# A hybrid decoder layer: late loads of the delta rule one tile further on, and the sparse branch's first items in another order

## The reference

```python
h = rmsnorm(x); u = h @ w_in
A = conformer_conv(u)                 # causal depthwise conv, w = 31
B = gated_deltanet(u)                 # chunked delta rule, 4 heads of 128
C = sparse_attention(u)               # 8 heads of 64 in 2 groups
x += (sigmoid(gA)*A + sigmoid(gB)*B + sigmoid(gC)*C) @ w_o
x += cross_attention(rmsnorm(x), mem)
x += relu(rmsnorm(x) @ w_ff1)**2 @ w_ff2
```

## Time and profile before

| what | us |
|---|---|
| median of three runs | 2863.49 |
| the three runs | 2863.49, 2866.32, 2855.11 |
| the profiled execution, its own time | 2858.21 |
| its span, first to last instruction | 2856.6 |
| TensorE matmuls busy in it | 2657.9 (93%) |
| VectorE, ScalarE, GpSimd busy | 1311.3, 853.5, 693.3 |
| mean granted clock of TensorE | 0.962 of 2.4 GHz |

### The profile page before, as it was taken

How to read it: one execution, slowest core, us unless ns; L and a number is a source line. 1 busy time by engine, 2 the same in 40 slices (tenths; PEclk the granted TensorE clock), 3 DMA queues, 4 the chain that set the end, 5 groups by cost and what they waited for, 6 DMA issues and landing times. The chain is left out here.

```text
span 2856.6 us, 53065 instructions
## 1 busy us (share of the span) xinstructions
PE 2657.9 (93%) x21974; PEld 2438.0 (85%) x21974; DVE 1311.3 (46%) x2318; ACT 853.5 (30%) x1603; POOL 693.3 (24%) x548
## 2 busy tenths in 40 slices
PE   8999999999889987888879999999999999999996
PEld 7999999999867764545548899988999999999995
DVE  4999999313133346455543352234333323324234
ACT  4333111123122234556652222135221121220221
POOL 1222222212143330121203424201422222222233
PEclk9999999999978897999999999999999999999998
DMA  5121252332386735335316551233111111111111
GB/s 176 53 60 60 98 107 87 92 98 70 110 256 197 212 104 204 119 110 161 119 43 224 145 188 60 74 132 134 48 44 50 45 45 45 45 45 46 50 46 61
DMA packets 148834, 290.35 MB, mean 102 GB/s; under 512 B 28100, under 2 KB 96648, under 8 KB 145842
## 3 DMA queue, kind: packets, MB, share of 16 engines
q1 hardware_dynamic: 136930, 255.48, 28.6%
q0 software_dynamic: 11520, 31.47, 3.5%
q10 hardware_dynamic: 144, 0.00, 0.0%
HBM read 245.94 MB, written 51.93 MB: 104 GB/s over the span
## 5 line engine op out<-in xcount | busy, mean ns | idle before, releaser
L165 POOL TENSOR_TENSOR mlp_w_low<-mlp_w_raw,mlp_w_high 128x1024 fp32r<-128x1024 f32 x72 | 174.5, 2424 | 656.8 <-ACT mlp_w_high L161 656.8
L362 PE MATMUL in_psum<-x_high,in_w_high 128*128 128x352 f32 x1416 | 264.5, 328 | 23.8 <-DVE x_low L557 13.8
L165 POOL TENSOR_TENSOR in_w_low<-in_w_raw,in_w_high 128x1024 fp32r<-128x1024 f32 x59 | 145.4, 2465 | 576.1 <-ACT in_w_high L161 576.1
L2759 PE MATMUL mlp_psum<-mlp_in,mlp_w_high 128*128 128x352 f32 x1536 | 264.9, 324 | 0.0
L161 ACT ACTIVATE mlp_w_high<-mlp_w_raw 128x1024 fp32r<-128x1024 f32 x72 | 76.4, 1061 | 624.2 <-PE mlp_psum L2759 624.2
L362 PEld LDWEIGHTS in_psum<-x_high,in_w_high 128*128 128x128 f32 x1416 | 234.4, 189 | 32.4 <-issue 17.0
L362 PE MATMUL in_psum<-x_low,in_w_high 128*128 128x352 f32 x1416 | 261.8, 327 | 0.0
L362 PE MATMUL in_psum<-x_high,in_w_low 128*128 128x352 f32 x1416 | 259.0, 324 | 0.0
L2759 PEld LDWEIGHTS mlp_psum<-mlp_in,mlp_w_high 128*128 128x128 f32 x1536 | 251.2, 189 | 0.2
L362 PEld LDWEIGHTS in_psum<-x_low,in_w_high 128*128 128x128 f32 x1416 | 237.3, 191 | 0.0
L362 PEld LDWEIGHTS in_psum<-x_high,in_w_low 128*128 128x128 f32 x1416 | 235.1, 190 | 0.0
(11 more groups left out here) (468 smaller groups left out, 4444.8 us busy)
## 6 DMA issues: line engine op xcount, KB each, us to landing
mlp_w_raw<-in_w_mlp SPq DMA_DIRECT2D x64, 512.0 KB, 3.5
in_w_raw<-in_w_in SPq DMA_DIRECT2D x59, 512.0 KB, 4.3
nsa_ring<-in_cache_slc SPq DMA_DIRECT2D x144, 128.0 KB, 3.9
u_scratch<-stage SPq DMA_DIRECT2D x32, 528.0 KB, 5.3
gdnp_page_ring<-in_cache_cmp POOLq DMA_DIRECT2D x128, 128.0 KB, 4.6
gdnp_page_ring<-in_cache_cmp SPq DMA_DIRECT2D x128, 128.0 KB, 4.8
nsa_ring<-in_cache_slc POOLq DMA_DIRECT2D x112, 128.0 KB, 4.1
aux<-u_scratch SPq DMA_DIRECT2D x24, 528.0 KB, 4.2
```

The source lines that it names most:

```text
L165: self.nc.gpsimd.tensor_tensor(self.low[:, i % 2, 0:k * P], self.raw[:, i % 2, 0:k * P], self.high[:, i % 2, 0:k * P].bitcast(F32), ALU.su ...
L362: return mm(psum[:, e % 2, n, 0:WN], w[:, i % 2, c * P:(c + 1) * P], a[:, c, n * WN:(n + 1) * WN], start=x == 0 and c == 0, stop=x == 2 an ...
L2759: return mm(psum[:, e % 2, n, 0:WN], w[:, i % 2, c * P:(c + 1) * P], a(c)[:, column(n)], start=x == 0 and c == 0, stop=x == 2 and c == CHU ...
```

## The change

In the delta rule, GpSimd and SyncE load four page steps first (FIRST = 4), then GpSimd's memsets, first mask product and padding and SyncE's new tokens follow, and then steps 4 and 5. The spill and the sample's inputs move into SyncE's loop at t = 1, behind that tile's token load and ahead of its pages. The transfer of `sample_mask` is gone.

In the sparse branch, the causal mask comes from `sample_consts`: `SC_OWN` has 16 columns instead of 4, `SC_EDGE` four more, and VectorE adds the latter to the window's bias; TensorE's three products with `early.mask` are gone. The past's scores go to banks 4 and 5, so that the 16 transposes wait for less. The preamble's new tokens, importance and past values become functions, called after the scoring of items 0, 1 and 2; ScalarE's and VectorE's counterparts move likewise. Head 0 takes tiles 0 to 7 in order. Both windows come first among the sets. `compare` moves behind item 2 and keeps only the small sums; its large comparisons stand behind items 4 (`larger`) and 6 (`equal`, with the tie-breaking), `count` behind 7, and `masks` before item 9.

```diff
-    STEPS, RING = N_PAGES // 4, 6
+    STEPS, RING, FIRST = N_PAGES // 4, 6, 4
...
+            def load_late():
+                sp.dma_start(spill, conv).then_inc(sent, 16)
+                sp.dma_start(own[:, :], t_dram["sample_own"]).then_inc(own_in, 16)
+                sp.dma_start(state_s[:, :, :, :], t_dram["state_gdn"]).then_inc(state_in, 16)
...
-            for step in range(RING):
+            for step in range(FIRST):
                 load_pages(sp, step, (0, 1), pages_in)
             sp.dma_start(qkv_new[:, :, :], qkvs[:, :, TP:W].rearrange("k p n -> p k n")).then_inc(sample_in, 16)
             sp.dma_start(zs[:, :, :], u[T_Z:T_Z + H, :, TP:W].rearrange("h p n -> p h n")).then_inc(sample_in, 16)
-            sp.dma_start(spill, conv).then_inc(sent, 16)
...
+            for step in range(FIRST, RING):
+                load_pages(sp, step, (0, 1), pages_in)
             for t in range(NT):
                 if t + 2 < NT:
                     load(t + 2)
+                if t == 1:
+                    load_late()
...
-            for step in range(RING):
+            for step in range(FIRST):
                 load_pages(pool, step, (2, 3), pages_in_pool)
...
             last.then_inc(pad_ready, 1)
+            for step in range(FIRST, RING):
+                load_pages(pool, step, (2, 3), pages_in_pool)
...
-    sets = [(x, hf, c) for hf in range(2) for x, c in [(WIN, 0)] + [(SLC, c) for c in range(NCH)]]
+    sets = [(WIN, 0, 0), (WIN, 1, 0)] + [(SLC, hf, c) for hf in range(2) for c in range(NCH)]
-    RANKED = 6
+    RANKED = 9
-        items.append((PROMPT, n // NT, (0, 7, 1, 6, 2, 5, 3, 4)[n] if n < NT else n % NT))
+        items.append((PROMPT, n // NT, n % NT))
...
-                mm(ps[:, b, 0:c1 - c0], early.rbx[:, :], early.hot[:, c0:c1], start=True, stop=False)
-            for k, at in enumerate((C_WIN, C_WIN + WINDOW, C_DIFF + PAGE)):
-                last = mm(ps[:, at // BANK, at % BANK:at % BANK + TS], early.mask[:, 0:P], early.mask[:, P + k * TS:P + (k + 1) * TS],
-                          start=False, stop=k != 1)
+                last = mm(ps[:, b, 0:c1 - c0], early.rbx[:, :], early.hot[:, c0:c1], start=True, stop=True)
...
                 for which, (n, k) in merged(scoring, tailing):
                     (tail if which else score)(n, k)
+                if i == 0:
+                    new_tokens()
+                if i == 1:
+                    importance()
+                if i == 2:
+                    past_values()
...
+            V.tensor_tensor(bias[:, C_WIN:C_WIN + TS], bias[:, C_WIN:C_WIN + TS], piece(SC_EDGE, TS), ALU.add)
...
                 if i >= 1:
                     scales(i - 1)
+                if i == 0:
+                    past_shares()
                 if i == 1:
+                    new_tokens()
+                if i == 2:
                     compare()
-                if i == 3:
+                if i == 4:
+                    larger()
+                if i == 6:
+                    equal()
+                if i == 7:
                     count()
```

More of the change, by code:

```diff
@@ L1516, in sparse @@
     last_of_head = {r: i for i, (kind, r, _) in enumerate(items) if kind == PROMPT}
-    last_set = {hf: item_of_set[hf * (NCH + 1) + NCH] for hf in range(2)}
+    last_set = {hf: item_of_set[1 + (hf + 1) * NCH] for hf in range(2)}
     def spans(tt):
@@ L1782, in _ @@
                 last.then_inc(v_turned, 1)
-            pe.wait_ge(turned, 1)
-            pe.wait_ge(past_ready, 2)
-            for b in range(4):
-                last = mm(ps[strip(b), M1, 0:NCMP], piece(SC_SUM, 32), sc[:, b % 2, :], start=True, stop=True)
-            last.then_inc(imp_mm, 1)
-            for hf in range(2):
-                tr(ps[:, 4 + hf, P:2 * P], sc[:, hf, :], ident[:, :]).then_inc(past_turned, 1)
-            for hf in range(2):
-                pe.wait_ge(past_pt, hf + 1)
-                for b in range(HB):
-                    last = mm(ps[strip(b), 4 + hf, 0:P], pt[:, hf, 0, strip(b)], vc_past[:, hf * HB + b, :], start=True, stop=True)
-                last.then_inc(past_pv, 1)
@@ new lines, in importance, with past_values @@
+            def importance():
+                pe.wait_ge(turned, 1)
+                pe.wait_ge(past_ready, 2)
+                for b in range(4):
+                    last = mm(ps[strip(b), M1, 0:NCMP], piece(SC_SUM, 32), sc[:, b % 2, :], start=True, stop=True)
+                last.then_inc(imp_mm, 1)
+                for hf in range(2):
+                    tr(ps[:, 4 + hf, P:2 * P], sc[:, hf, :], ident[:, :]).then_inc(past_turned, 1)
+            def past_values():
+                for hf in range(2):
+                    pe.wait_ge(past_pt, hf + 1)
+                    for b in range(HB):
+                        last = mm(ps[strip(b), 4 + hf, 0:P], pt[:, hf, 0, strip(b)], vc_past[:, hf * HB + b, :], start=True, stop=True)
+                    last.then_inc(past_pv, 1)
+                pe.wait_ge(past_out, 2)
+                tr(ps[0:NC, 4, 0:P], vct[:, :], ident[:, :]).then_inc(vc_turned, 1)
+                pe.wait_ge(m0_read, 1)
@@ L1882, in _ @@
             act.wait_ge(v_turned, 2)
-            act.activation(vtok[:, 1, :, :], ps[:, 2:4, :], ACT.Copy).then_inc(v_ready, 1)
+            act.activation(vtok[:, 0, :, :], ps[:, 0:2, :], ACT.Copy).then_inc(v_ready, 1)
+            for i in range(LAG - 1):
+                for _ in exps(i):
+                    pass
+                if i == 0:
+                    act.wait_ge(turned_mm, 1)
+                    act.activation(vn[:, :, :, :].rearrange("p a b n -> p (a b n)"), ps[0:NEW, M1, :], ACT.Copy).then_inc(turned, 1)
             for hf in range(2):
@@ L1891, in _ @@
             act.activation(vc[:, :], ps[0:NC, 4, 0:P], ACT.Copy).then_inc(vc_ready, 1)
-            for i in range(LAG - 1):
-                for _ in exps(i):
-                    pass
             for i in range(LAG, NI + LAG):
@@ L2054, in _, with past_shares @@
+            def past_shares():
+                for hf in range(2):
+                    dve.wait_ge(past_exp, hf + 1)
+                    V.reciprocal(inv[:, hf:hf + 1], sums_s[:, hf:hf + 1]).then_inc(inv_ready, 1)
+                    dve.wait_ge(inv_ready, hf + 1)
+                    V.tensor_scalar(sc[:, hf, :], sc[:, hf, :], inv[:, hf:hf + 1], None, ALU.mult).then_inc(past_ready, 1)
             row = score[:, :].unsqueeze(1).to_broadcast([P, IH, NBLK])
```

125 lines of the change are left out of this document (55 added, 70 removed).

## The result

The changed kernel takes 2871.03 us (median of 8 runs, 2862.87 to 2872.61), the kernel before 2861.02 (8 runs beside them, 2855.11 to 2866.32). The range ended at 2868. By the 0.5% that the chances go by it is "the same" (0.63), but the interval lies wholly above 1, so the sign is clear, and it is the other one.

A forecast was written before the change was run, and what follows sets the result against it. TensorE was taken as the bound nearly everywhere. From the profiled 2858.2 us, 5 for the delta rule and 5 for the sparse branch gave 2848; the median's 5.3 above that execution made it 2853, range 2838 to 2868.

The forecast's parts named there:

- GpSimd's two steps: Delta rule's start: two page steps issued later start the first tile 2.2 us earlier; 2 us allowed for their late landing.
- Late loads out of the first tile: First tile: 5.1 MB fewer removes TensorE's 4.58 us stall and half clock; tile ends at about 811 instead of 823.1.
- rival D: First tile: the stall is not a matter of DMA load and comes again with its half clock; 2857 us, chance 0.08.
- rival B: Second tile: the stall only moves there, 4.6 us plus 24 us at half clock; 2858 us, chance 0.13.
- The late loads in the second tile: SyncE's queue: they take 14 us, step 14 goes out at 829 to 835, TensorE waits 4 to 10 us.
- rival E: Second tile: step 14 lands 10 us later, after 850; TensorE waits 17 us, half clock follows; 2878 us, chance 0.08.
- Delta rule: 5 us gained: Second tile ends at 846 instead of 851.0, everything after shifted by that; 834.5 at best, 853 at worst.
- Masks and first score: Sparse branch's start: first score bound by head 0's late biases, so at most 3 us earlier than 1099.36.
- The first head's chain: Sparse branch's start: VectorE's chain takes 12.7 us, to 1109.1, TensorE's moved pieces lie beside it; 6.6 us gained.
- Taken back: about 2 us of scoring, and up to 2.: First head: small items scored first leave about 2 us more scoring; the first comparison holds the fifth item up to 2.
- Head 2's query load: Sparse branch, sign of being right: this load comes 10 us earlier than its 1201.
- The signs named in the prediction: If right: second-tile page wait 4 to 10 us, third tile at 843 to 849, no VectorE wait above 4 before fourth item.

The follow-up runs named there:

- e4: Kernel before with only the page-step edit: four steps first, two behind the sample's loads, late loads still in the first tile; 2865.15 us (ratio 1.0006).
- e1: Kernel before with both delta-rule edits (four page steps first, late loads in the second tile), sparse branch as before; 2865.33 us (ratio 1.0009).
- e3: Kernel before with only the late loads moved, as a block, to the second tile; all six page steps first; 2864.66 us (ratio 1.0010).
- e10: Kernel before, spill in four parts behind page steps of the second to fifth tile, state and small inputs behind the last page step; 2857.56 us (ratio 0.9988).
- e12: The delta rule of e10 with the sparse branch of e11; 2858.57 us (ratio 0.9993 to the kernel before).
- e5: Kernel before with the late loads as sixteen transfers, one behind each page step from the second tile on; 2864.15 us (ratio 1.0009).
- e9: Kernel before with the late loads as one block behind the second tile's page steps and gate load; 2864.03 us (ratio 1.0017).
- e8: Kernel before with head 0 in natural order and the ranking spread over items, preamble still ahead of the first score; 2861.31 us (ratio 1.0001).
- e11: Changed kernel with the delta rule of before and the preamble, except past values' products, ahead of the first score again; 2860.93 us (ratio 1.0001).

## Why the prediction was wrong, step by step

*GpSimd's two steps.* The start of the first tile was right in kind (787.53 forecast as 788.5). The 2 us allowed for the two late steps were too little: e4 loses 5.1 in the tile for the 3.0 of the earlier start. With the late loads out of the tile, nothing is left of the 2.2 either (815.7 and 815.0 against 813.9 to 815.1).

*Late loads out of the first tile.* Right in mechanism. The stall by issue goes with the DMA engines' load where it falls. The longest of the first tile is 2.83 to 4.58 us in the seven kernels with the late loads there, 1.15 to 1.53 in the five without them and with six steps first, and 3.00 and 2.20 in the changed kernel and e1. The long ones begin between 799.4 and 803.6; the changed kernel's row for that stretch, and e3's, in which no stall is longer than 1.48 us:

```profile
799.00:803.00 4.00, 1.00 (x61) 0.73 (x52) 0.48 (x1) 1.34 (x5) 2.82 (x5) 0.84 1.07 337
```

```profile
799.00:803.00 4.00, 4.00 (x182) 3.40 (x181) 1.90 (x5) 1.55 (x6) 1.71 (x4) 0.95 0.45 143
```

The share is full with the stall and 0.45 without it (0.46 in e10, 0.60 and 0.64 in e12 and e5); e3's 1.48 us come later, at 809, where the share is 1.03. In the changed kernel it is the two moved page steps and the sample's loads that fill it. That takes rival D away, under which the stall would have stayed in e3 and e10.

What TensorE waits for can be read from the trace. The page of the kernel before has among its DMA queues (packets, MB, share) and its busy times:

```profile
PE 2657.9 (93%) x21974; PEld 2438.0 (85%) x21974; DVE 1311.3 (46%) x2318; ACT 853.5 (30%) x1603; POOL 693.3 (24%) x548
...
q8 instruction: 174, 2.85, 0.4%
```

The 174 packets have 16,384 bytes each, 65 for each of TensorE's 43,948 instructions, and come as TensorE goes on: this queue is its instruction stream. In the fourteen traces (the two kernels' and the twelve runs') TensorE stands still by issue for more than 1 us 52 times, and each time it goes on 1.2 to 1.7 us after such a packet has come in, though in that phase the packets come at least 3.3 and mostly 4 to 6 us apart. In the first tile before, the packet of 802.72 came 7.4 us after the one ahead of it (795.31), and the stall ended at 805.06; in e3 they come 3.5 to 4.0 us apart there. So the prediction's "its instructions arriving late through busy DMA engines" is right.

Of rival B a part is true. In the changed kernel TensorE stands still by issue for only 1.66 us in the second tile, not 4.6, and the low clock stands around the page wait; but e9 has its 3.52 in the third tile, where its block goes out. The Trainium skill, in Runtime: NRT & Kernel Launch, Instruction fetch mechanics, holds that the streaming of instructions is mostly hidden; over the whole kernel that agrees (three stalls above 1 us for 174 packets before), but beside full DMA engines it was not hidden here, by up to 4.58 us. The tile ended at 815.67, not 811, for the reason above (*GpSimd's two steps*): it took 28.1 us and not 22.5.

*The late loads in the second tile: the step that failed.* "The late loads then take what they took before, 808.34 - 794.32 = 14 us." They took 20.7. In the kernel before, the spill's issue was 0.50 us and only the one-hot table's was held (6.42); in the second tile the spill was held too, for 7.03 (7.00 in e3), `own` behind it for 2.54 and the table for 5.94 (8.82 in e3, 10.82 in e9). So the time for which an issue holds the queue is a matter of the place, not of the transfer, and a sum from one place doesn't carry to another. One such place was in the earlier trace rows: the first issue behind a tile's token load (L747). Before, that is step 14's, and the pair of steps that it opens takes 9.56 us, where the next pair takes

```profile
849.03 2.95 SPq L739 DMA_DIRECT2D gdnp_page_ring<-in_cache_cmp  x4
```

In all fourteen traces that issue is held for 4.5 to 7.0 us from the second tile on, whatever it carries, but for one of 0.99 in e9, behind its block. The late loads were put right into that place, so the spill took the 7.03, and the 14 us, read where nothing of the kind stands ahead, were short by about that. The one-hot table is held wherever it stands in the block, and for 0.39 us in e5, behind a page step and a piece of the bias table. Why an issue is held there the rows don't say. Step 14 went out at 845.20 instead of 829 to 835 and was there at 851.35, past both of rival E's points, "after about 845" and "after 850". E was the right mechanism, with its half clock (20.5 us), and priced too high: a wait of 7.85 and not 17, 9.6 us worse than the forecast at the third tile's start and not 21. Its 0.08 was far too low: 6.7 us in one term made it the outcome, and that term (14 us, or 7.6 unblocked) had been given a better end and none worse than its row. That the wait of 7.85 lies in the forecast's "4 to 10" is luck: the page came 8 us and more after the forecast 837 to 843, and TensorE, in a tile that began 4.7 late and with 6.8 us at the low clock from 815.4, asked for it at 843.5 and not at 833.

*"Delta rule: 5 us gained."* Even with the queue right it is not sure: e10 and e12, with one delta rule, have the third tile 9.2 and 9.3 us early, and the supply of pages takes back all but 1.3 and 5.7 by the sample's tile (e9's gain goes in its block). The changed kernel shows the other side: 4.6 late at the third tile and level at the seventh. I priced a gain at the third tile as a gain at the end ("everything after shifted by that"), although showed TensorE already waiting for a page in the next tile. (The best case's sum, 811 - 2 + 24.8 + 1, is 834.8 and not 834.5.)

*Masks and first score.* Right. The first score is bound by head 0's biases; it came 13.2 us after the branch's first product instead of 15.4, so 2.2 earlier, of 3 at most.

*The first head's chain: the second step that failed.* "TensorE's own moved pieces (some 5 us) lie beside it." Where the pieces are not there, the fourth item's score comes 12.3 (e8) and 12.4 us (e11) after the first. That is close to the chain's 12.7, but partly by luck: 1.6 of these were past shares and new tokens' copies, which stand ahead in both, so the chain to compare is 11.1, some 1.2 us short. With the pieces it takes 16.7. VectorE's chain waits for the second and third item's scores, TensorE does moved products ahead of each, and at the low clock they are 6.8 us (1.02 + 1.04 + 1.89 ahead of the second item, 0.65 + 0.69 ahead of the third, 1.08 + 0.40 ahead of the fourth). Ahead of the first score they cost the 2 to 3 us by which it came later and no more, for head 0's biases were late anyway. The forecast had this cap in its hand and used it on one side only.

*"Taken back: about 2 us of scoring, and up to 2."* Too small as well. e8 has the fourth item's score 4 us sooner after the first and the third output 10.5 sooner (31.9 against 42.4), and the tenth output at the same time (101.5 against 101.7): with the large tiles last, the stretch from the sixth to the tenth output takes 41.4 us instead of 31.9. The order moves work within the head and takes none away.

Head 2's query load, too, follows the tenth output, so it comes 7 us later and not 10 earlier. The signs named in the prediction did show the fault: a page wait of "4 to 10 us at the second tile's seventh group" is what came (7.85), but the third tile at 855.6 and not 843 to 849; no wait on VectorE above 4 us before the fourth item, but that item no sooner.

## What to carry to other kernels

A transfer moved in a queue is to be costed by how long its issue can be held there, with the worst held issue of the trace as the bad end, by what stands right ahead of it, and by the first load behind it. Where every later tile shows a wait of a few us for the same supply, a gain in one tile is not a gain at the end. Work that is done ahead of a late load is free as far as it ends before the load comes: moved behind it, it lay on the path here, and at the lower clock. And a stall that no semaphore explains may be found in the trace's DMA queues, among them the instructions' own.

## What the runs showed of the hardware

- One issue on SyncE's queue held it for 0.3 to 10.82 us, the same transfer in different places: the spill 0.50 (before), 1.70 (e9), 7.00 (e3), 7.01 (e1) and 7.03 (changed kernel), the one-hot table of 389 KB 0.39 (e5), 5.94 (changed kernel), 6.42 (before), 8.21 (e1), 8.45 (e12), 8.73 (e10), 8.82 (e3) and 10.82 (e9).
- The first issue behind a tile's token load was held for 4.5 to 7.0 us in every trace from the second tile on (0.99 once, in e9), the one behind it mostly for 0.35.
- TensorE's stalls "by issue" of more than 1 us, 52 in fourteen traces, each ended 1.2 to 1.7 us after a 16,384-byte packet of the DMA queue "instruction" (q8) had come in. In the first tiles in which the DMA engines were full between 799 and 803 the longest was 2.20 to 4.58 us.
- In the changed branch TensorE ran at 0.50 from 1098.7 to 1122.6; the wait of 7.64 us ended at 1101.86, and of the next 14.1 us it was busy for 13.2. In the second tile it ran at 0.50 from 842.7 to 863.2, with the wait of 7.85 us up to 851.35 in it.
